# First layer of a three-block transformer kernel: two convolved projections computed side by side, their weight slabs interleaved by chunk, one modulation unit moved behind them

## The reference, cut to what matters

```
mod = silu(c) @ w_ada + b_ada               # 6 parts: sh1, sc1, g1, sh2, sc2, g2
h = rms_norm(x) * (1 + sc1) + sh1
proj = h @ w_in                             # q_a, k_a, v_a, qk_m (1024 wide), v_m, o_m, gates
qk_m = silu(causal_conv(qk_m, conv_w, conv_b))   # the two convolved projections, 512 columns each
q_m, k_m = split(qk_m)
gates = gates + b_gate                      # 8 columns: input and forget gates of the mLSTM
hm = mlstm(q_m, k_m, v_m, gates) ...
```

## Time and profile before

| | |
|---|---|
| median of 3 runs | 1299.81 us (1299.56 to 1300.06) |
| profiled execution: time | 1299.54 us |
| profiled execution: span in the profile | 1297.7 us |
| PE busy | 1117.4 us, 86% of the span |
| DVE busy | 670.3 us, 52% |
| ACT busy | 549.5 us, 42% |
| DMA | 397.36 MB, mean 306 GB/s |

### The profile page before, as it was taken

How to read it: one execution, slowest core, us unless ns; L and a number is a source line. 1 busy time by engine, 2 the same in 40 slices (tenths; PEclk the granted TensorE clock), 3 DMA queues, 4 the chain that set the end, 5 groups by cost and what they waited for, 6 DMA issues and landing times.

```text
span 1297.7 us, 20055 instructions
## 1 busy us (share of the span) xinstructions
PE 1117.4 (86%) x8501; PEld 843.3 (65%) x8501; DVE 670.3 (52%) x1422; ACT 549.5 (42%) x1202; POOL 0.2 (0%) x4
## 2 busy tenths in 40 slices
PE   6999999877666675757889999999999979999997
PEld 5777668644343442424556677888887758888886
DVE  4565766211110111111167756998876867777765
ACT  4554553211111110111155665666654755666653
POOL 0000000000000000000000000000000000000000
PEclk9999999998798887889899999999999989999999
DMA  9996848999999999999997457667757615544510
GB/s 389 421 428 273 364 193 327 428 426 427 427 426 428 422 427 426 428 427 427 425 420 285 161 216 280 241 271 294 289 224 292 234 60 201 198 190 190 194 33 33
DMA packets 29703, 397.36 MB, mean 306 GB/s; under 512 B 3496, under 2 KB 4904, under 8 KB 5416
## 3 DMA queue, kind: packets, MB, share of 16 engines
q1 hardware_dynamic: 29176, 395.72, 74.6%
q10 hardware_dynamic: 432, 0.30, 0.1%
HBM read 394.97 MB, written 1.05 MB: 305 GB/s over the span
## 4 chain that ended last, share of the span: by engine, by line
PE 56%; DMA 23%; DVE 12%; ACT 6%; issue 2%; DVEq 0%; SPq 0%; ACTq 0%
PE ps L1214 17%; DMA ring<-in_w13b 15%; PE ps L1218 9%; PE ps L1208 4%; PE ps L1210 4%; PE ps L1209 4%; DVE memr L2491 4%; DMA mem<-in_w 4%; ACT mem L1972 3%; PE ps L1764 3%; DVE mem L2491 3%; PE ps L1248 3%; DMA mem<-in_w13b 2%; ACT memr L1972 2%; PE ps L1724 2%
## 5 line engine op out<-in xcount | busy, mean ns | idle before, releaser
L2491 DVE TENSOR_TENSOR memr<-ring,memr 128x512 fp32r<-128x512 f32 x432 | 292.4, 690 | 158.0 <-ACT memr L1972 154.6
L1972 ACT ACTIVATE memr<-ring 128x512 fp32r<-128x512 f32 x432 | 265.2, 629 | 187.8 <-PE ps L1210 78.1
L1214 PE MATMUL ps<-memr 128*128 128x512 f32 x1056 | 275.4, 394 | 3.3 <-DVE memr L2491 2.0
L1972 ACT ACTIVATE mem<-ps 128x256 f32<-128x256 f32 (+5 forms) x294 | 121.5, 432 | 344.2 <-PE ps L1764 226.6
L1214 PEld LDWEIGHTS ps<-memr 128*128 128x128 f32 x1056 | 186.9, 189 | 36.4 <-DVE memr L2497 5.0
L1208 PE MATMUL ps<-memr 128*128 128x256 f32 (+2 forms) x504 | 175.6, 348 | 4.6 <-DVE memr L2491 3.4
L2491 DVE TENSOR_TENSOR mem<-mem,ps 128x512 f32<-128x512 f32 (+1 forms) x76 | 43.5, 573 | 238.8 <-ACT mem L1972 238.8
L1210 PE MATMUL ps<-memr 128*128 128x256 f32 (+2 forms) x504 | 165.2, 328 | 0.0
L1209 PE MATMUL ps<-memr 128*128 128x256 f32 (+2 forms) x504 | 165.0, 327 | 0.0
L1218 PEld LDWEIGHTS ps<-memr 128*128 128x128 f32 x1056 | 151.5, 190 | 16.5 <-DVE memr L2497 0.9
L1218 PE MATMUL ps<-memr 128*128 128x256 f32 x1056 | 157.0, 282 | 0.9 <-DVE memr L2497 0.5
(11 more groups left out here) (190 smaller groups left out, 1006.7 us busy)
## 6 DMA issues: line engine op xcount, KB each, us to landing
ring<-in_wpk SPq DMA_DIRECT2D x89, 2048.0 KB, 8.6
ring<-in_w13a SPq DMA_DIRECT2D x17, 2048.0 KB, 45.5
mem<-in_w13b SPq DMA_DIRECT2D x16, 2048.0 KB, 46.0
ring<-in_w SPq DMA_DIRECT2D x16, 2048.0 KB, 46.1
ring<-in_w13b SPq DMA_DIRECT2D x16, 2048.0 KB, 43.9
mem<-in_w SPq DMA_DIRECT2D x15, 2048.0 KB, 45.2
mem<-in_w13a SPq DMA_DIRECT2D x15, 2048.0 KB, 45.5
mem<-in_wpk SPq DMA_DIRECT2D x1, 2048.0 KB, 10.4
```

Source lines behind the costliest of these rows:

```text
L1214: return self.e.matmul(ps[:, 0:512], a[0], b[1], start=start, stop=stop)
L1972: return self.e.activation(out, src, f, **k)
L2491: return self.e.tensor_tensor(out, a, b, op)
```

## The change

The slabs of `conv0` and `conv1` are taken in turn: both for chunk 0, both for chunk 1, and so on. So the host lays the two units out anew (`tile_in`): the unit that comes first holds the eight slabs of chunks 0 to 3, the other those of chunks 4 to 7. All of the first unit is now used in `first_half`, with `ada(0, 1)` and `ada(0, 3)` after its first four slabs. The second one moves ahead of `ada(0, 4)` in the order of loads, and the products of `ada(0, 4)` move behind both projections and the gates. `conv(0)` joins the side jobs only after all 16 slabs.

```diff
-    mixed(ada(0, 0), ada(0, 2), (U_IN + 3, 8), ada(0, 1), ada(0, 3), ada(0, 4), (U_IN + 4, 8), ada(0, 5), (U_IN + 6, 8),
+    mixed(ada(0, 0), ada(0, 2), (U_IN + 3, 8), ada(0, 1), ada(0, 3), (U_IN + 4, 8), ada(0, 4), ada(0, 5), (U_IN + 6, 8),
...
-            if split and 0 < c < 4:
-                self.stage(1)
+            if split and 0 < c < 3:
+                self.stage(2)
...
-    conv_step = p.project_T_steps("conv0", m.h2, low((0, 0)), 256, 128)
+    conv_steps = [p.project_T_steps(f"conv{u}", m.h2, low((0, 0)), 256, 128) for u in range(2)]
 
     def first_half():
         p.warm(4, low((0, 0))(0))
-        for _ in range(4):
-            next(conv_step)
-        p.ada_mm(0, 1)
-        p.ada_mm(0, 3)
-        p.ada_copy()
-        p.ada_close(True)
-        p.ada_mm(0, 4)
+        for k in range(4):
+            for step in conv_steps:
+                next(step)
+            if k == 1:
+                p.ada_mm(0, 1)
+                p.ada_mm(0, 3)
+                p.ada_copy()
+            if k == 2:
+                p.ada_close(True)
 
     p.pad_conv()
-    p.modulate_x(0, 0, "n0", {4: first_half, 7: p.ada_copy})
-    for _ in conv_step:
-        pass
+    p.modulate_x(0, 0, "n0", {4: first_half})
+    for k in range(4):
+        for step in conv_steps:
+            next(step)
+    p.last = p.spent - 1
     p.conv_copy(0)
     p.gate_weights()
     p.jobs.append(p.conv(0))
     p.side.append(p.work())
-    p.project_T("conv1", m.h2, low((0, 0)), 256, 128)
     p.conv_copy(1)
     p.gates()
     p.jobs += [p.conv(1), p.gate_rows()]
-    if not p.side:
-        p.side.append(p.work())
+    p.ada_mm(0, 4)
+    p.ada_copy()
     p.ada_unit(0, 5)
...
+def tile_in(w):
+
+    t = tile_cols(w[:, 0:3584])
+    t[3:5] = t[3:5].reshape(2, 128, 8, 512).transpose(2, 0, 1, 3).reshape(2, 8, 128, 512).transpose(0, 2, 1, 3).reshape(2, 128, 4096)
+    return t
```

More of the change, by code:

```diff
@@ L3420, in build @@
             [tile_ada(i["w_ada"][0], 0), tile_ada(i["ada_w_2"][0], 1), tile_ada(i["ada_w_2"][1], 2),
-             tile_cols(i["w_in"][0][:, 0:3584]), tile_list(i["w_out"][0], [(4, 8), (0, 4)]),
+             tile_in(i["w_in"][0]), tile_list(i["w_out"][0], [(4, 8), (0, 4)]),
              tile_pairs(i["a_w_qkv_2"][0][:, 0:2048]), tile_cols(i["a_w_qkv_2"][0][:, 2048:3072]),
```

## The result

| | before | after |
|---|---|---|
| median of 6 runs each, same chip | 1299.99 us (1299.56 to 1301.18) | 1309.58 us (1308.71 to 1312.79) |
| ratio | | 1.0074, 95% interval 1.0064 to 1.0084 |
| profiled execution: time, span | 1299.54, 1297.7 us | 1309.97, 1308.1 us |

The changed kernel is 9.6 us slower by the medians, and 10.4 us between the two profiled executions. Forecast were 8.3 us, 1307.8 us in all, with a range of 1303.2 to 1310.8.

The account below looks back on a forecast made before the run. The prediction saw a long DMA-set stretch whose start is delayed by whatever delays PE in the first layer's mixer. Terms 5.1 + 1.8 + 1.4 = 8.3 us on 1299.54 gave 1307.8 us; range 1303.2 to 1310.8, forecast's own 1305.5 to 1309.5.

Parts of the forecast that it names:

- Step 1: First eight slabs: two run per chunk of h, gaining 1.6 us by s3; s7 ends at 41.1 us.
- Step 2: Behind s7: PE has nothing for 3.2 us until chunk 4 of h is made; s8 starts at 44.3 us.
- Step 3: Gates wait 4.4 us for weights behind om's splits; om starts at 66.8 us, before 61.7: first term +5.1 us.
- Step 4: At q0: late side jobs push the gates' row work, so PE waits: second term +1.8 us, bounds 0 and 3.
- Step 5: Behind the two waits the clock falls; only the second fall costs: third term +1.4 us, bounds 0 and 1.7.
- Rival E: More than one clock fall that counts, or one in the wait at q0 too: 1310 us and more; chance 0.06.
- Step 6: From om to the experts and the end: the whole shift arrives, 8.3 us, giving 1307.8 us.
- Rival D: Expert stretch, set by DMA, starts no later, so the delay is given back: no change, 1299.5 us; chance 0.05.
- Rival C: Without both waits, by another queue order, om's landing alone holds PE: 4.1 us gained, 1295.4 us; chance 0.05.

Follow-up runs that it names:

- e1: Changed kernel, splits of the second unit's first four slabs written behind chunks 5 and 6 of h, two behind each; 1310.58 us, ratio 1.0080.
- e10: Changed kernel with the edits of e3 and e6 together; 1302.05 us, ratio 1.0011.
- e5: Changed kernel with unused identity products filling PE's waits for chunk 4 of h and ahead of the gates; 1309.62 us, ratio 1.0069.
- e7: Kernel before, with only conv(0) joined to the side jobs after both projections; 1305.95 us, ratio 1.0038.
- e11: Changed kernel with the edits of e3 and e5 together; 1305.18 us, ratio 1.0032.
- e2: Changed kernel, split of the gate weights written early, ahead of the splits of om; 1307.37 us, ratio 1.0058.
- e3: Changed kernel, seven more side-job steps written directly behind the gates; 1305.94 us, ratio 1.0037.
- e6: Changed kernel, products of ada(0, 4) and ada(0, 5) moved ahead of the gates, only PE's order edited; 1306.61 us, ratio 1.0046.
- e12: e9 with the splits of vm also held back until the end of om; 1297.26 us, ratio 0.9972 to the kernel before.
- e4: Changed kernel with the edits of e1, e2 and e3 together; 1301.17 us, ratio 1.0005.
- e9: Changed kernel with e1's edits, early gate weights, and om's splits held back until the gates and three side steps are written; 1300.24 us, ratio 0.9993.
- e8: Kernel before, with only ada(0, 4) moved, in loads behind conv1's unit and on PE behind the gates; 1303.94 us, ratio 1.0021.

## Why the prediction was right, and where its sizes were off

| | forecast | after | what the runs say |
|---|---|---|---|
| Step 1, s7 ends | 41.1 us | 41.11 | |
| Step 2, wait for chunk 4 | 3.2 us | 3.10 | worth nothing while the second wait stands (e1); counts, with the clock behind it, where the other two are gone (e10) |
| Step 3, gates wait, `om` starts | 4.4 us, 66.8 | 3.40, 68.92 | 66.82 when the clock is kept up (e5) |
| Step 4, wait at `q0` | 1.8 us | 2.79 | 3.7 by itself (e7) |
| Step 5, clock | 1.4 us | in `om`'s 68.92 | 1.6 ahead of `om` (e5, e11) |
| sum | +8.3 us | +9.6 by medians, +10.4 between the profiled executions | |

**Steps 1 to 3 held**, to 0.1 us for the first two. The replay of the queues in their new order gave the two waits, their releasers and, for the first, its size. Within step 1, s3 ended at 31.0 and not 30.6 us, which did not matter, because the landing of `ada(0, 3)` set the next start. The gates' wait is shorter than forecast only because the low clock behind the first wait had pushed s15 from 55.9 to 57.5 us; step 5 had said so. The gates began at 60.87 against 60.3 us. The load of `om` ended ACT's wait 0.4 us later than in the earlier trace rows (56.62 for 56.26), and ACT then waited another 0.47 us for a DVE instruction (L2497) that the sum had left out. The landing of that load moves by itself: it ended ACT's wait at 55.80 us in e1 and at 56.62 after. The weights' place in the queue is shown as the cause of the wait by e2, which moves only that.

**Step 4 was mis-sized.** Its term was +1.8 us and it measured 2.8 in the profile after. The step took the split released by `vm`'s seventh slab to end at V - 0.65. It ended at V + 0.3, because on ACT it stood behind a last activation of the convolution that waited 1.13 us for DVE's taps (in e7 at V + 1.2, behind the same piece). I had counted the row work of the gates and left out the end of `conv(1)` that stands in front of it. e7, with no load late, waits even longer, so the hole in the loads behind the gates is not needed to explain this; whether it adds to it was not separated. e3 shows the whole term to be recoverable: the steps fit into the 8.75 us in which DVE was idle.

**Step 5 held** in the traces. Both falls came where they were expected. The first cost nothing in the end, though only as long as a second wait hid it (1.6 us in e6 and e10). The second cost 1.6 us ahead of `om` (e5, e11), where I took 1.4 with a bound of 1.7. That this arrives in the time is not shown: the medians of e3 and e11 are not told apart. What the step did not have is a fall at the third wait. In the profile after there was none, but in those of e1, e2, e5, e6 and e7 there was one, worth 1.5 to 2.3 us each time. In e5 it swallowed 1.6 of the 2.1 us that had been gained. That it also spreads the times of one kernel (1308.7 to 1312.8 us after) is likely but was not shown. Rival E had named it, at 0.06 (1310 and more).
The Trainium skill, "TensorE: Matmul & The Clock Gate", section "What's actually happening", says that how many slow products a kernel sees at its start changes from run to run. Here the traces show the same in the middle of one: behind the same wait of 3.10 us, and with the same code up to there, products ran at the lower clock in the profile after (0.59 and 0.56) and at full clock in that of e2.

**Step 6 held**: +10.05 us at 103 us and +10.05 us in the expert stretch. Rival D (given back later) falls with it, and e12 shows the same in the other direction, 3.0 us early at `q0` and 3.5 us less in the end.

**Rival C** (faster, were the queues in another order) was close to what could be had. It named 4.1 us, with the splits behind chunks 4 to 7 and the gate weights ahead of `om`'s splits. Built in e4 and e9 it gave nothing, since the same trap stood one stage on, in `om` and in `vm`; e12 takes that away too and has 3.5 us. The loss is thus not in interleaving the slabs. Most of it is in what `stage()` writes in front of the work that PE waits for next, and the rest in the side jobs that begin late (e7).

The chances have a small slip: forecast and rivals add up to 0.90 slower and 0.05 faster, where the text says 0.89 and 0.06.

## What to carry to other kernels

On an engine that works strictly in order, a prefetch step which waits for a load or for a distant slab is a barrier for everything behind it: write first what the next engine needs, and stage the splits of the next unit only when its load is about to land. Before an edit is dropped or praised, look for who is idle beside the wait: here DVE had 8.75 us free, and work moved into them gave back the whole wait of 2.8 us at `q0`. Remove waits together, since a later one swallows what an earlier one gives back (in e1 the slabs ended 5 us earlier and the gates waited 7.54 us for 3.40), and read each step's trace for the next wait.

## What was unexpected of the hardware

The length of a wait on PE did not decide whether the granted clock fell. After 2.18 us (e9) and 2.24 us it fell, and after 2.39 us (e8) and 2.79 us (`q0` in the profile after) it did not. After 3.10 us it fell in the profile after and in those of e3, e6 and e10, and not in e2's. A fall cost 1.5 to 2.3 us of PE time under dense products.
